# Re-ordering the first block of a three-block transformer kernel: half of the modulation moved into the attention, residual and router turned feature-major

## The reference, cut to what matters

```python
sh1, sc1, gt1, sh2, sc2, gt2 = adaln(c, w_mod, b_mod)       # silu(c) @ w_mod + b_mod, 6 x 1024 columns
csh1, csc1, ...              = adaln(c_ctx, w_mod, b_mod)
hl, hc = rmsnorm(xl) * g_mix * (1 + sc1) + sh1, the same of xc with csc1, csh1
k, v   = keys_values(hl and hc);  q = queries(hl)           # w_in, 1792 columns
mix_l  = concat(gqa_attend(q, k, v), spatial_gating(hl))    # 8 heads, 512 keys
x      = xl + gt1 * (mix_l @ w_out)
h      = rmsnorm(x) * g_ffn * (1 + sc2) + sh2
aff    = softmax(h @ w_router)                              # 16 experts
gate, idx = top_k(aff.T, 32);  xe = h[idx]                  # each expert takes 32 tokens
x      = x + gt2 * scatter(gate * (silu(xe @ w1) * (xe @ w3)) @ w2)
```

## Time and profile before

| | |
|---|---|
| median of 3 runs | 3077.66 us (3073.49 to 3084.65) |
| the profiled execution, its time | 3079.64 us |
| its span | 3077.9 us |
| TensorE busy | 2787.0 us (91% of the span), 14677 matmul records |
| VectorE, ScalarE, GpSimd busy | 532.1, 355.3, 66.8 us |
| mean granted TensorE clock | 0.885 |
| moved by DMA | 695.25 MB, mean 226 GB/s |

### The profile page before, as it was taken

The page is one execution under the profiler, slowest core; times in us unless marked ns, Lnnn a source line. Parts: engine busy times, 40 slices in busy tenths (PEclk is TensorE's granted clock), DMA queues, the critical chain, the costliest instruction groups (busy, mean ns, idle before and its releaser), DMA issues. The chain is left out here.

```text
span 3077.9 us, 34693 instructions
## 1 busy us (share of the span) xinstructions
PE 2787.0 (91%) x14677; PEld 2108.3 (69%) x14677; DVE 532.1 (17%) x1138; ACT 355.3 (12%) x788; POOL 66.8 (2%) x81
## 2 busy tenths in 40 slices
PE   5877888878888888999998899999999997899999
PEld 1764444435435444788887788888888886688888
DVE  0222100100100010211113421111111123421111
ACT  1121010101101011000002210100000102301000
POOL 0000000000000000000010000000000010000000
PEclk8867877877786777899998899999999998899999
DMA  9701899999999999744554134344444553134440
GB/s 375 246 26 69 360 422 422 422 422 422 422 422 422 421 422 422 262 157 143 174 144 151 50 102 162 126 147 154 150 156 145 172 146 124 55 123 145 152 154 28
DMA packets 278456, 695.25 MB, mean 226 GB/s; under 512 B 15985, under 2 KB 197473, under 8 KB 229089
## 3 DMA queue, kind: packets, MB, share of 16 engines
q1 hardware_dynamic: 275760, 688.56, 59.9%
q10 hardware_dynamic: 2608, 5.44, 0.5%
HBM read 692.90 MB, written 1.05 MB: 225 GB/s over the span
## 5 line engine op out<-in xcount | busy, mean ns | idle before, releaser
L997 PE MATMUL banks<-ZT,ring 128*128 128x256 f32 x2816 | 624.2, 380 | 1.3 <-ACT ZT L1464 1.3
L997 PEld LDWEIGHTS banks<-ZT,ring 128*128 128x128 f32 x2816 | 535.7, 190 | 74.8 <-issue 1.8
L895 PE MATMUL banks<-ring,BK 128*32 128x512 f32 x2048 | 294.8, 699 | 108.4 <-DMA ring<-in_w 89.6
L1013 PE MATMUL banks<-ZP,ring 128*128 128x256 f32 x1408 | 317.0, 379 | 0.0
L1013 PEld LDWEIGHTS banks<-ZP,ring 128*128 128x128 f32 x1408 | 267.5, 190 | 36.4
L895 PEld LDWEIGHTS banks<-ring,BK 128*32 128x32 f32 x2048 | 57.5, 115 | 326.2 <-DMA ring<-in_w 205.3
L1197 PE MATMUL banks<-ZT,ring 128*128 128x256 f32 x1024 | 241.5, 391 | 0.0
L1197 PEld LDWEIGHTS banks<-ZT,ring 128*128 128x128 f32 x1024 | 200.5, 198 | 28.0
L1900 DVE TENSOR_TENSOR ZP<-banks,RB 128x512 f32<-128x512 f32 x88 | 60.8, 691 | 686.9 <-PE banks L997 686.8
L707 PE MATMUL banks<-ring,ZT 128*128 128x256 f32 (+2 forms) x832 | 175.9, 374 | 2.3 <-ACT ZT L1333 1.1
L707 PEld LDWEIGHTS banks<-ring,ZT 128*128 128x128 f32 x832 | 155.8, 198 | 22.7 <-ACT YT L1333 1.5
(11 more groups left out here) (319 smaller groups left out, 1934.7 us busy)
## 6 DMA issues: line engine op xcount, KB each, us to landing
ring<-in_w SPq DMA_DIRECT2D x384, 1024.0 KB, 20.8
ring<-in_w_in SPq DMA_DIRECT2D x79, 1024.0 KB, 5.0
ring<-in_ffn_w_gate SPq DMA_DIRECT2D x44, 1024.0 KB, 5.3
ring<-in_ffn_w_up SPq DMA_DIRECT2D x44, 1024.0 KB, 7.7
ring<-in_ffn_w_down SPq DMA_DIRECT2D x44, 1024.0 KB, 4.8
ring<-in_w_mod SPq DMA_DIRECT2D x24, 1024.0 KB, 15.4
ring<-in_w_branch SPq DMA_DIRECT2D x16, 1024.0 KB, 5.1
ring<-in_w_out SPq DMA_DIRECT2D x12, 1024.0 KB, 4.9
```

The costliest lines, as they stand in the source:

```text
L895: last = mm(ps[32 * j:32 * j + 32, 4 + b, :], XE[:, k, :], slot(n)[:, 512 * b:512 * b + 512], start=(k < 4), stop=(k >= 4))
L997: last = mm(ps[:, 4 + q % 4, 256 * w:256 * w + 256], slot(n + w)[:, 256 * k + P * (q % 2):256 * k + P * (q % 2) + P], ZT[:, k, :], start=( ...
L1013: last = mm(ps[:, c // 2, 256 * (c % 2):256 * (c % 2) + 256], slot(n + 2)[:, D * (q % 2) + P * c:D * (q % 2) + P * c + P], FH[:, q % 4, :] ...
```

## The change

The order of the first block is rewritten. Nothing is changed after the gather, but for the numbering of the stages (one more root-mean-square stage of the later kind, so counts go up by one).

1. **Order of the loads.** `w_mod` blocks 0 to 3 (shift and scale of the first norm), then `w_in`, then blocks 4 to 11, `w_out`, router, experts. On ACT's queue the identity comes first, alone; x and context come ahead of the rest of the constants; the two `b_mod` broadcasts are gone.
2. **Modulation.** All twelve blocks give columns (also the gates). Blocks 4 to 11 are done one in each attention unit, after the turn, in bank 7; their sum is one unit later, ahead of the turn. The unit's weighted values share bank 6.
3. **Norms.** x is turned unnormed into `XT`, at once; both norms are turned between the first four blocks and copied out plain; scale and shift are applied in SBUF as soon as the four blocks are summed (`affine`), and the first tile's matmuls wait chunk by chunk.
4. **Projection and residual** are feature-major: eight output chunks of 128 features, 8 matmuls of 256 tokens each, the chunk outermost. One DVE instruction per chunk does `XT += gt1 * projection`.
5. **Norm and router.** `RZ = XT * gain`; the router multiplies `RZ`, and its result is scaled by rstd and has a bias added (`BR`, the shift times `w_router`, from eight matmuls ahead of `turn_y`). The squares are summed as in the later layers: ACT squares, GpSimd adds, two matmuls. The tokens for the gather are `XT` turned back (16 transposes) and scaled by rstd into `Z`.

The core of the diff:

```diff
-U_WIN = 24
+U_WIN = 8
+U_MODB = 15
+def mod_unit(m):
+    return U_MOD + 2 * m if m < 4 else U_MODB + 2 * (m - 4)
@@ SyncE
+            for ch in range(4):
+                mod(ch)
             for u in range(7):
                 cols256(U_WIN + u, w_in, 256 * u)
+            for ch in range(4, 12):
+                mod(ch)
@@ TensorE
+            mod_part(0)
+            (16 transposes of X).then_inc(x_turned, 1)
+            mod_part(1)
+            pe.wait_ge(const_in, 32)
+            mod_sum(0)
             norm(0)
+            mod_part(2)
+            mod_sum(1)
             norm(1)
-            normed(1)
+            mod_part(3)
+            mod_sum(2)
+            mod_sum(3)
+            pe.wait_ge(modcols_out, 1)
@@ attention, per unit
                     if i + 1 < len(units):
                         score(i + 1, units[i + 1])
+                    if first:
+                        first(i)                  # mod_sum(3 + i), for i > 0
                     turn(i, unit)
-                    if between:
-                        between(i)
+                    between(i)                    # mod_part(4 + i)
                     weigh(i, unit)
@@ TensorE, ahead of turn_y
+            for k in range(KC):
+                last = mm(ps[:, 7, 16:16 + NE], BB[:, k, :], slot(U_ROUTER)[:, NE * k:NE * k + NE], ...)
+            last.then_inc(bias_full, 1)
@@ projection
-            project_out(U_WOUT, 0, ZT)
-            norm(2)
-            normed(2)
-            tok_tile(ZT, U_ROUTER, 4, NE).then_inc(unit_done, 1)
+            for c in range(KC):
+                for k in range(KC):
+                    last = mm(ps[:, 4 + c % 4, 256 * (c // 4):256 * (c // 4) + 256],
+                              slot(U_WOUT + k // 2)[:, D * (k % 2) + P * c:D * (k % 2) + P * c + P], ZT[:, k, :], ...)
+                    if c == KC - 1 and k % 2:
+                        last.then_inc(unit_done, 1)
+            for c in range(KC):
+                pe.wait_ge(xt_new, c + 1)
+                (2 transposes of XT[:, c])
+            square_sums(0)
+            for k in range(KC):
+                zg_chunk(0, k)
+            tok_tile(RZ, U_ROUTER, 4, NE).then_inc(unit_done, 1)
@@ ScalarE, per attention unit
                     pt_copy(i)
+                    if first:
+                        part_copy(4 + i)
@@ VectorE, per attention unit
+                    if first and i:
+                        mod_columns(3 + i)
                     pt_copy(i)
@@ VectorE, after the projection
-            gated_update(0, 4)
-            scaled(2, X)
-            norm_out(2, ZT, col(scaleA, 2), col(scaleB, 2))
+                stt(out=XT[:, c, :], in0=ps[:, 4 + c % 4, ...], scalar=gt1[:, c:c + 1], in1=XT[:, c, :],
+                    op0=ALU.mult, op1=ALU.add).then_inc(xt_new, 1)
+                gained(0, c, RZ, lambda c: scaleA[:, 2, c:c + 1])
```

More of the change, by code:

```diff
@@ L529, in _, with mod @@
             w_mod = a["w_mod"][0]
[L530 to L533, removed]
+            def mod(ch):
+                for half in range(2):
+                    n = mod_unit(ch) + half
+                    load(n, slot(n).rearrange("p (k n) -> p k n", k=4),
+                         w_mod[512 * half:512 * half + 512, 512 * ch:512 * ch + 512].rearrange("(k p) n -> p k n", p=P))
+            for ch in range(4):
+                mod(ch)
             w_in = a["w_in"][0]
@@ new lines, in mod_sum @@
+            def mod_sum(m):
+                pe.wait_ge(part_copied, m + 1)
+                bank, c0 = (6, 8 * m) if m < 4 else (7, 0)
+                for n in range(4):
+                    last = mm(ps[:, bank, c0 + 2 * n:c0 + 2 * n + 2], PART[m % 2][:, P * n:P * n + P], C("pick"),
+                              start=True, stop=True)
+                last.then_inc(modcols_full, 1)
+            def norm(v):
+                if v:
+                    pe.wait_ge(norm_out_a, 2)
+                    pe.wait_ge(norm_out_v, 2)
+                else:
+                    pe.wait_ge(xt_copied, 4)
@@ L739, in _, with attention @@
                 last.then_inc(turn_full, 1)
-            def attention(units, base, scores, between=None):
+            def attention(units, base, scores, between, first=None):
                 def turn(i, unit):
@@ new lines, in part_copy, with affine @@
+            def part_copy(m):
+                wait_done(act, mod_unit(m) + 1)
+                fn(PART[m % 2], ps[:, 4 + m % 2 if m < 4 else 7, :], ACT.Copy).then_inc(part_copied, 1)
+            def affine(v, dst):
+                for c in range(0, KC, 2):
+                    fn(dst[:, c, :], dst[:, c, :], ACT.Identity, scale=scaleA[:, v, c:c + 1], bias=scaleB[:, v, c:c + 1]
+                       ).then_inc(lhs_a, 1)
+            act.wait_ge(cols_copied, 1)
+            fn(cs, vcol[:, V1["c"]:V1["c"] + 16], ACT.Silu).then_inc(c_silu, 1)
@@ L1349, in _ @@
[L1349 removed]
+            part_copy(0)
+            act.wait_ge(x_turned, 1)
+            act.wait_ge(norm_scaled, 2)
+            for b in (0, 2):
+                fn(XT[:, 2 * b:2 * b + 2, :], whole(b), ACT.Copy).then_inc(xt_copied, 1)
+            part_copy(1)
+            norm_out(0, ZT)
             act.wait_ge(ctx_in, 16)
             squares(1, XC)
[L1352 removed]
+            part_copy(2)
+            norm_out(1, CT)
@@ L1647, in _, with affine @@
-            dve.wait_ge(affine_set, 5)
-            def col(table, i):
-                return lambda c: table[:, i, c:c + 1]
-            norm_out(0, ZT, col(scaleA, 0), col(scaleB, 0))
-            scaled(1, XC)
-            norm_out(1, CT, col(scaleA, 1), col(scaleB, 1))
+                    copy(dst[:, 2 * b:2 * b + 2, :], whole(b)).then_inc(norm_out_v, 1)
+            def affine(v, dst):
+                for c in range(1, KC, 2):
+                    ts(dst[:, c, :], dst[:, c, :], scaleA[:, v, c:c + 1], scaleB[:, v, c:c + 1], ALU.mult, ALU.add
+                       ).then_inc(lhs_v, 1)
@@ new lines, in _ @@
+            scaled(0, X)
+            dve.wait_ge(x_turned, 1)
+            dve.wait_ge(norm_scaled, 2)
+            for b in (1, 3):
+                copy(XT[:, 2 * b:2 * b + 2, :], whole(b)).then_inc(xt_copied, 1)
+            norm_out(0, ZT)
+            scaled(1, XC)
+            norm_out(1, CT)
+            dve.wait_ge(modcols_full, 4)
+            tt(modc[:, 0:16, :], ps[:, 6, 0:32].rearrange("p (c w) -> p c w", w=2),
+               over(vcol[:, V1["b_mod"]:V1["b_mod"] + 16], 2), ALU.add).then_inc(modcols_out, 1)
@@ new lines, in _ @@
+            dve.wait_ge(modcols_out, 1)
+            for w in range(2):
+                stt(out=scaleA[:, w, :], in0=modc[:, 8:16, w], scalar=1.0, in1=vcol[:, V1["g_mix"]:V1["g_mix"] + 8],
+                    op0=ALU.add, op1=ALU.mult).then_inc(affine_set, 1)
+            copy(scaleB[:, 0:2, :], modc[:, 0:8, :].rearrange("p c w -> p w c")).then_inc(affine_set, 1)
+            dve.wait_ge(affine_set, 3)
+            dve.wait_ge(norm_out_a, 4)
+            affine(0, ZT)
+            affine(1, CT)
```

370 lines of the change are left out of this document (180 added, 190 removed).

## The result

The changed kernel takes 2989.89 us (median of four, 2984.76 to 2990.18) against 3079.22 us of the kernel before run beside it: a ratio of 0.971, 95% interval 0.969 to 0.973. It is faster, as forecast. The profiled execution has a span of 2988.1 us, 89.8 less than before.

A forecast was written before the change was run, and what follows sets the result against it. It took `w_mod` loads to bound the start, gaps and clock the attention, loads the experts, TensorE the rest. Six terms summed to -67.2 us by an earlier first expert, forecasting 3010.5 us from the 3077.66 median, range 2995 to 3040.

The forecast's parts named there:

- Terms 3 and 6: From last weigh to projection: +2.5 us (0 to +6); from softmax to first expert: -3.3 us (-4 to -2).
- Rival 2: The experts' loads are late because SP's queue is held in the attention: up to 3040 us; chance 0.07.
- Rival 3: Each attention unit becomes one serial chain of 19.7 us, making the kernel slower than before: 3102 us; chance 0.02.
- Rival 4: No change, the experts' stream being set by something that does not move: 3078 us; chance 0.01.
- term 2: Attention stage: +1.3 us, at the full clock with one slow unit (-4.7 at full clock throughout, +41 at the half).
- term 4: Projection: 0 us change (-0.5 to +1).
- Term 1: Start to first `w_in` tile: from 101.3 to 47.5 us, -53.8 us (-59 to -52).
- Term 5: From the projection to the end of the router: -13.9 us (-15.6 to -11.3).
- Rival 1: The attention falls to the half clock and stays, so its stage gets 41 us longer: 3050 us; chance 0.15.

The follow-up runs named there:

- experiment 5: The changed kernel with the contraction index k outermost in the projection, so that all chunks end together: 2998.41 us (one run).
- experiment 6: The changed kernel with norm(0) moved ahead of modulation block 1 and norm(1) ahead of block 2: 2999.22 us, ratio 0.9737 to the kernel before.
- experiments 7 to 9: The changed kernel with norms sooner, bias-column copy before the gating, four loads later: 2985.35 us; with copy and loads only: 2983.95; with copy only: 2989.60.
- experiment 1: The kernel before with eight added 512-column matmuls per attention unit, results unused, and units sharing bank 6: 3062.74 us against 3075.99, ratio 0.9956.
- experiment 2: The changed kernel with all twelve modulation blocks and their loads back ahead of the tiles: 3047.95 us, ratio 0.990 to the kernel before.
- experiment 3: The changed kernel with the matmuls of blocks 4 to 11 moving 2 columns instead of 512: 3013.34 us (one run).
- experiment 4: The kernel with narrow blocks 4 to 11, plus sixteen transposes of the identity in place of each block: 2986.25 us (one run).

## Why the prediction was wrong in its size, and where it was right

**Right.** The whole gain came from the earlier start of the first expert, and the experts' stage did move as a block: 950.4 us against 951.6. Terms 3 and 6 came out within 0.5 us. Rival 2 (late loads) was wrong: the first expert's wait ahead of it is for its gathered tokens, not for weights. Rival 3 (a serial chain) was wrong: 6.75 us a unit, far from the 16.6 at which it decides. Rival 4 fell with the result.

**The step that failed is term 2, in its size.** I forecast the attention 1.3 us longer, and it came out 9.3 us shorter. The choice of the full clock held, but I gave away what it is worth in two ways, both on the safe side.
- I added the durations of the five steps (1.13, 1.05, 1.09, 2.12, 1.97) to 7.4 us. But neighbouring records overlap, by 0.07 to 0.13 us in the timeline after, and the block takes 1.93 us as one, not 2.12 as two halves. From start to start the steps are 1.05, 0.92, 1.00, 1.85, 1.93, together 6.75. The stage without a slow unit came to 59.7 by my sum, and took 55.1: 4.6 us.
- I took one unit at the half clock for the beginning (+6.0). In the profiled execution no record of the attention is slow. Seven profiles have the blocks in full in the attention (the changed kernel twice, and experiments 5 to 9). In four of them part of unit 0 is slow, and it costs 1.6 us (first turn to second score 6.43 instead of 4.81), not 6.

Together these are the 10.6 us.

**The range was too narrow as well.** Even with every term at its best bound my sum gives -83.8 us, a time of 2993.9, and 2989.89 was measured. The attention at -9.3 lies below its best bound of -4.7, and the projection (term 4) at -1.9 below its -0.5. The stages without a term, which I put at nothing, made 6.3 us: tiles 2.2, the wait ahead of the projection 0.9, the way to the first expert 1.9, the rest 1.3.

**What the constants depend on.** It isn't the attention's clock.
- *Tiles.* The first 96 records take 20.96 us instead of 23.19. But they take 20.96 in experiment 1 too, where nothing ahead of them was edited, and 22.64 in the second profile of the changed kernel. This 2.2 differs between executions and can't be put down to the change.
- *Projection.* Its new form takes 28.51 us in the changed kernel and 28.40 in experiment 2, where attention and gating had the lower clock. In the changed kernel it starts out of a turn at the half clock (3.75 us, as before). What differs is that there is no wait between turn and projection (0.69 before). In windows of 2 us, the clock reaches 1.00 by 178, 3 us into the projection, and by 246 in the kernel before, 5 us into it. That this comes from the missing wait is my reading; no run tests it.
- *Gather.* It takes 3.99 us instead of 6.66, but 4.04 in experiment 2, and from 3.76 to 6.15 over the profiles of experiments 5 to 9. Why is open.

**Term 1** was too cautious by 2.5 us: I put the end of the chain at 47.5 within 42.2 to 49.4; it was 45.0, and between 43.4 and 43.9 in five other profiles with the same start. **Term 5** fell on its best bound: the router ran at 3.73 us, and transposes, square sums and router follow on each other and on 28 us of projection with waits of no more than 0.2 us. The router's part of it isn't certain in every execution: it takes 3.73 or 3.72 in five profiles with the same code there, and 5.47 in experiment 6.

**Rival 1 and the rule of the Trainium skill.** I had given 0.15 to a fall to the half clock. Experiment 3 is that case, and it came about by taking the wide matmuls out of the unit. The unit there is 10.1 us, not 13.4, since its block is narrow. The Trainium skill, "TensorE: Matmul & The Clock Gate", Part 4, would have transposes not count as TensorE being busy; experiment 4, where sixteen added transposes take the unit from 10.09 to 6.88 us, disagrees for float32 transposes. The same page of the Trainium skill, Part 1, says that the number of matmuls at the lower clock at a kernel's start varies between runs of one kernel; here the first unit in mid-kernel varies in this way (1.09 and 1.66 us for the same turn in two executions).

What stays open: why the last sums of the start, the first tiles, the first unit and the gather are at the half clock in some executions and not in others; why a router without waits ahead of it was slow in experiment 6; and how the 19.9 us behind the attention in experiment 2 are split among the parts of the new layout, beyond the 3 to 5 us of experiment 5.

## What to carry to other kernels

Where a stage waits a little in every step, look first at its clock. Filling the waits with wide work from elsewhere can pay twice, since here the old work then ran at the full clock, and so did the gating right behind it in experiment 1. Move loads into stages where the DMA engines idle, and count the move by the units it takes from in front of the critical stage. For a sum of gapless steps take distances from start to start, not durations. Give a stage that you hold constant a range too: the same tiles took 20.96 and 22.64 us in two executions of one kernel. And before calling a stage shorter because of a clock, look for an experiment without that clock that has the same stage.

## What was not expected of the hardware

- Fifteen us of added matmuls made a kernel 13 us faster (experiment 1), and about twelve us of removed ones made another 24 us slower (experiment 3, one run).
- The half clock (0.53 in the stage) held while TensorE was busy for 9.6 of each 10.1 us, with score, sums and transposes and 2-column and 64-column matmuls between them (experiment 3); with sixteen more transposes in the unit the stage ran at 0.97 and the unit took 6.88 us.
- Moving two groups of 16 transposes one place ahead, with no work added, came with a median 12 us higher (experiment 6). But one of its five runs, at 2988.90, is within the range of the unmoved kernel, and the first kernel of experiments 7 to 9 has the same move and a median of 2985.35, so the move isn't shown to be the cause. In the profile (its slowest run) the first expert is 7.4 us later, and the experts and the later layers are 2.6 and 3.1 us longer. Of the 2.6, 2.2 are one group of 16 records at the end of the last expert, which takes 5.87 us instead of 3.69; for the 3.1 I have no cause.
